# A one-core transformer kernel: the last expert phase fetches an expert's down and up row as one 8 KB row, in groups of four ranks over eight places

## What is computed

```python
def one(args):                      # 128 tokens at a time
    hh, ee, gg = args               # tokens, expert numbers, gates
    a = jnp.einsum("tkd,td->tk", peer_down[ee], hh)
    act = (gg * jax.nn.gelu(a)).astype(hh.dtype)
    return jnp.einsum("tk,tkd->td", act, peer_up[ee])
```

## Time and profile before

| | us |
|---|---|
| median of three runs | 3842.82 |
| lowest and highest run | 3831.79, 3847.68 |
| span of the profiled execution (its own time) | 3996.2 |
| x1's expert phase in it, first gather to the first use of the last sum | 2140.55 to 2909.40 |
| mean DMA rate in that stretch | 359 GB/s |

### The profile page before, as it was taken

One profiled execution on the slowest core, in us unless ns is written; L12 is line 12 of the kernel. 1 busy time (PEld: TensorE's weight loads), 2 busy tenths in 40 slices (PEclk: granted clock), 3 DMA queues, 4 the chain that ended last, 5 costly groups with the idle time before them and its releaser, 6 DMA issues. The chain is left out here.

```text
span 3996.2 us, 45598 instructions
## 1 busy us (share of the span) xinstructions
PE 2820.0 (71%) x15322; PEld 1797.2 (45%) x15322; DVE 2411.0 (60%) x5173; ACT 925.2 (23%) x2085; POOL 1518.1 (38%) x1757
## 2 busy tenths in 40 slices
PE   5999676778664545676686534434489979999999
PEld 2587332324341231222254200000079869798798
DVE  3445788455558776455456776565455766565565
ACT  2432111220111111111131100111133633334433
POOL 0001566665646656666503666666600000000000
PEclk7999887888877777788888766777689989999999
DMA  7666999999989999999926999999955315555444
GB/s 282 251 252 230 361 393 379 383 375 378 388 333 352 372 353 356 376 381 389 376 72 244 363 357 366 365 356 363 366 184 190 128 69 189 173 191 173 153 160 158
DMA packets 274190, 1157.02 MB, mean 290 GB/s; under 512 B 31057, under 2 KB 31825, under 8 KB 235602
## 3 DMA queue, kind: packets, MB, share of 16 engines
q0 software_dynamic: 221184, 805.40, 52.9%
q1 hardware_dynamic: 52818, 349.25, 24.2%
HBM read 1153.49 MB, written 1.05 MB: 289 GB/s over the span
## 5 line engine op out<-in xcount | busy, mean ns | idle before, releaser
L1181 PE MATMUL ps<-rows,diag 128*32 128x512 f32 x3072 | 830.4, 779 | 891.5 <-DMA rows<-in_peer_up,iup 701.7
L2242 DVE CUSTOM_DVE_ANT_0 rows<-rows,ps 128x1024 f32<-128x1024 f32 x768 | 924.6, 1220 | 512.9 <-DMA rows<-in_peer_down,idown 416.3
L2731 POOL DMA_INDIRECT rows<-in_peer_down,idown x768 | 732.7, 954 | 548.6 <-PE ps L1181 322.9
L2731 POOL DMA_INDIRECT rows<-in_peer_up,iup x768 | 732.0, 953 | 318.0 <-issue 208.4
L1181 PEld LDWEIGHTS ps<-rows,diag 128*32 128x32 f32 x3072 | 141.3, 125 | 1519.8 <-DMA rows<-in_peer_up,iup 1214.0
L1243 PE MATMUL ps<-hT_hi,w_hi 128*128 128x256 f32 x1792 | 508.7, 284 | 9.1 <-DVE hT_lo L2383 9.1
L1245 PE MATMUL ps<-hT_lo,w_hi 128*128 128x256 f32 x1792 | 508.3, 284 | 0.0
L1244 PE MATMUL ps<-hT_hi,w_lo 128*128 128x256 f32 x1792 | 506.4, 283 | 0.0
L2806 POOL TENSOR_TENSOR ss<-nwt,minus_half 128x1 f32<-128x1 f32 x24 | 13.2, 551 | 1075.2 <-DVE nwt L1956 1075.2
L1243 PEld LDWEIGHTS ps<-hT_hi,w_hi 128*128 128x128 f32 x1792 | 343.2, 192 | 14.6 <-issue 13.6
L1244 PEld LDWEIGHTS ps<-hT_hi,w_lo 128*128 128x128 f32 x1792 | 342.7, 191 | 0.1
(11 more groups left out here) (327 smaller groups left out, 3899.1 us busy)
## 6 DMA issues: line engine op xcount, KB each, us to landing
wring<-in_wgu SPq DMA_DIRECT2D x66, 1024.0 KB
wring<-in_wdn SPq DMA_DIRECT2D x33, 1024.0 KB
wring<-in_wG SPq DMA_DIRECT2D x32, 1024.0 KB
wring<-in_wmod SPq DMA_DIRECT2D x29, 1024.0 KB
wring<-in_wpq SPq DMA_DIRECT2D x24, 1024.0 KB
rows<-in_wgu SPq DMA_DIRECT2D x22, 1024.0 KB, 4.9
rows<-in_wmod SPq DMA_DIRECT2D x19, 1024.0 KB, 7.6
rows<-in_peer_down,idown POOLq DMA_INDIRECT x768
```

Of the source, the lines that this page charges most:

```text
L1181: ins = pe.matmul(ps[qd:qd + QUAD, UPB + half, :], quad_w[:, j, :], rows[:, j, half * 512:(half + 1) * 512], start=(first and j < QUADS), ...
L2242: dve.tensor_tensor_reduce(out=rows[:, j, :], in0=rows[:, j, :], in1=h_ps, scale=1.0, scalar=0.0, op0=ALU.mult, op1=ALU.add, accum_out=a8[ ...
L2731: pool.indirect_dma_start(out=rows[:, j, :], out_offset=None, in_=table, in_offset=bass.IndirectOffsetOnAxis(ap=offs[:, j:j + 1], axis=0)) ...
```

## The change

- A new input table `peer1` holds layer 1's down and up row of an expert side by side (2048 numbers, 8 KB). In x1's phase one indirect DMA per rank fetches 128 of these rows (1 MB).
- Eight places of 8 KB (`both`): four in `rows`, three in `kvmem`, one in `h[1]` (the context's vectors). Groups of four ranks use places 0 to 3 and 4 to 7 in turn; a place is free again when the ups of its rank are done (`both_up`).
- DVE computes four downs, the gelu and the gates of four ranks (`both_downs`); ACT makes four full 128 x 128 diagonals (`both_diags`); PE multiplies a full diagonal with each half of the up row (`both_ups`), one group behind.
- Ranks are not moved among the partitions in x1 any more: the `moved` stages, the masked copies `sent`, the `move` products and the offset copies on POOL fall away there.
- Loops are written out in x1's phase. Stages that lay beside the first or second half of a group of eight now follow the DVE and ACT work of the first or second group of four; on PE they come ahead of the ups of the group before.
- The gain of the first feed-forward layer has another place; x0 and c0 are unchanged but for the tables' shapes.

```diff
+        both = [rows[:, 2 * n:2 * n + 2, :].rearrange("p a n -> p (a n)") for n in range(HALF)]
+        both += [kvmem[:, n * 2 * D:(n + 1) * 2 * D] for n in range(3)] + [h[1][:, :, :].rearrange("p t n -> p (t n)")]
...
+            def both_ups(i):
+                first, last = i % FOURS == 0, i % FOURS == FOURS - 1
+                if first:
+                    pe.wait_ge(sum_read, GATHER_NO["x1", i // FOURS])
...
+                for j in range(HALF):
+                    pe.wait_ge(both_diag, HALF * i + j + 1)
+                    s = HALF * (i % 2) + j
+                    for half in range(2):
+                        ins = pe.matmul(ps[:, UPB + half, :], diag[:, s, :], both[s][:, D + half * 512:D + (half + 1) * 512],
+                                        start=(first and j == 0), stop=(last and j == HALF - 1))
+                    ins.then_inc(both_up, 1)
...
+                if run == "x1":
+                    for part_, stages in enumerate((beside_a, beside_b)):
+                        i = FOURS * t + 2 * n0 + part_
+                        run_stages(stages)
+                        if i:
+                            both_ups(i - 1)
...
+            def both_diags(i):
+                cols = slice(HALF * (i % 2), HALF * (i % 2) + HALF)
+                act.wait_ge(both_g, 2 * i + 2)
+                act.activation(th8[:, cols], g2[:, cols], ACT.Tanh, scale=GELU_C).then_inc(both_tanh, 1)
+                act.wait_ge(both_act, 2 * i + 2)
+                for j in range(HALF):
+                    s = HALF * (i % 2) + j
+                    if i >= 2:
+                        act.wait_ge(both_up, HALF * (i - 2) + j + 1)
+                    act.activation(diag[:, s, :], ident[:, :], ACT.Copy, scale=act8[:, s:s + 1]).then_inc(both_diag, 1)
...
+            def both_downs(t, n):
+                i = FOURS * t + n
...
+                for j in range(HALF):
+                    c = HALF * (i % 2) + j
+                    dve.wait_ge(both_in[c], 16 * (i // 2 + 1))
+                    dve.tensor_tensor_reduce(out=both[c][:, 0:D], in0=both[c][:, 0:D], in1=h_ps, scale=1.0, scalar=0.0,
+                                             op0=ALU.mult, op1=ALU.add, accum_out=a8[:, c:c + 1]).then_inc(both_down, 1)
...
+            def gather_both(t):
+                for k in range(P):
...
+                    no, c = P * t + k, k % GROUP
+                    if no >= GROUP:
+                        pool.wait_ge(both_up, no - GROUP + 1)
+                    pool.indirect_dma_start(out=both[c], out_offset=None, in_=A["peer1"],
+                                            in_offset=bass.IndirectOffsetOnAxis(ap=idx[t][:, k:k + 1], axis=0)).then_inc(both_in[c], 16)
```

More of the change, by code:

```diff
@@ L33 @@
 HALF = GROUP // 2
+FOURS = P // HALF
 SLOTS = 3
@@ L78, in routes @@
 def routes(r, t, ks):
-    return [st for k in ks for st in [("route", r, t, k, 0), ("route", r, t, k, 1)] + [("moved", r, t, k)] * (k >= 8)]
+    return [st for k in ks for st in [("route", r, t, k, 0), ("route", r, t, k, 1)] + [("moved", r, t, k)] * (k >= 8 and r != "x1")]
 SETS = [[(0, 1), (1, 2), (2, 4), (4, 8)], [(0, 4), (4, 8)]]
 RANKS = [(0, 8, 1, 9, 2, 3, 10, 4, 5, 6, 7, 11), (0, 1, 2, 3, 8, 4, 5, 6, 7, 9)]
-SENDS = [(run, t, 8 + n) for run, t in GATHERS for n in range(len(SETS[t]))]
+SENDS = [(run, t, 8 + n) for run, t in GATHERS if run != "x1" for n in range(len(SETS[t]))]
 def set_mark(t, n):
@@ L135, in during @@
             m = n + 1
-            if not mine[2 * n] and not mine[2 * n + 1]:
+            if r != "x1" and not mine[2 * n] and not mine[2 * n + 1]:
                 while m < GROUPS and not mine[2 * m] and not mine[2 * m + 1]:
@@ L663, in build @@
             "idx_copied", "gelu_step", "gelu_in", "gelu_th", "act_ready", "diag_ready"))
+        both_in = [sem(f"both_in{n}") for n in range(GROUP)]
+        both_down, both_up, both_g, both_tanh, both_act, both_diag = (sem(n) for n in ("both_down", "both_up", "both_g", "both_tanh", "both_act", "both_diag"))
         slot_ok, exp_half, sum_read = sem("slot_ok"), sem("exp_half"), sem("sum_read")
@@ L2232, in gather @@
                 G = GATHER_NO[run, t]
+                if run == "x1":
+                    for part_, stages in enumerate((beside_a, beside_b)):
+                        both_downs(t, 2 * n0 + part_)
+                        run_stages(stages)
+                    return
                 def down(g, first=False):
@@ L2797, in gather @@
                     up(GROUPS - 1, 1, True)
-            for run, t in GATHERS:
-                gather(run, t)
+            def gather_both(t):
+                for k in range(P):
+                    if k % TOP == 0 and (sets := [n for n, (h0, _) in enumerate(SETS[t]) if TOP * h0 == k]):
+                        at_mark(pool, "route", "x1", set_mark(t, sets[0]))
+                    no, c = P * t + k, k % GROUP
[3 more added lines that the diff above has]
+                                            in_offset=bass.IndirectOffsetOnAxis(ap=idx[t][:, k:k + 1], axis=0)).then_inc(both_in[c], 16)
+            for run, t in GATHERS:
+                if run != "x1":
+                    gather(run, t)
+            pool.wait_ge(upp_done, 4 * P)
+            for t in range(TT):
+                gather_both(t)
             pool.memset(minus_half[:, :], -0.5).then_inc(half_set, 1)
```

79 lines of the change are left out of this document (56 added, 23 removed).

## The result

| | us |
|---|---|
| kernel before, median of five runs | 3837.84 |
| changed kernel, median of five runs (lowest, highest) | 3860.86 (3851.18, 3871.61) |
| ratio | 1.0051, 95% interval 1.0034 to 1.0068 |
| span of the profiled execution of the changed kernel | 3862.2 |
| x1's phase in it, first gather to the first use of the last sum | 2043.38 to 2776.70, 733.3 |

The change makes the kernel 0.5% slower where 3803 us, 1.0% faster, was forecast. The interval excludes 1, so the small loss is clear of noise. The profile alone seems to tell another story: its phase is 35 us shorter than the 768.9 of before, and near the forecast 728.2. But its phase also begins at 2043.38 where it began at 2140.55, after stages that the change leaves alone. So the two profiles were not comparable, and the first question is what an execution of the kernel before that takes 3840 us looks like.

What follows compares the result with a forecast made beforehand. The prediction took x1's expert phase as bound by DMA transfers with a small part of starvation. Its terms, 686.0 + 18.8 + 9.8 + 6 + 8.6 - 1.0, gave 728.2 us against 768.9, scaled to 3803 us, range 3755 to 3842.

Steps and rivals of the forecast that it cites:

- The baseline: Whole kernel: median is 0.9616 of the profiled span of 3996.2 us, so -40.7 us there becomes -39, 3803 us.
- The sum itself: x1's expert phase: ranks, side loads, start, DVE's lag and tail add up to 728.2 us, against 768.9 before.
- Starvation: x1's steady part before the change: the queue runs thin at share 0.97, where the best stretches reach 1.03.
- A place comes free in time: x1's groups of four: place free 4.9 us after last landing, new bytes at 7.9, queue dry at 10.7, 2.8 in hand.
- The clock: PE's bursts in x1: even starting each at half speed after about 3 us idle costs nothing or tenths of a us.
- Packets: x1's gathers: 8 KB packets at 335 ns and share 1.00, so 2.68 us a rank and 686.0 us for 256 ranks.
- cut rows: Rival in x1's gathers: rows are cut in two, 349 ns for 8 KB, 2.79 us a rank, 3830 us; chance 0.08.
- Tail: End of x1's phase: 10.5 us from last landing to first sum where it was 1.2, less 0.7, so +8.6 us.
- The thin queue: Rival in x1's transfers: share stays at 0.965, a rank takes 2.777 us, 3828 us; chance 0.10.
- Memory: Rival in x1's transfers: the mean rate is what memory gives to scattered rows, only the tail is added, 3850 us; chance 0.06.
- Half clock: Rival in x1's full products: PE stays at 1.2 GHz through the bursts, 3.74 us a rank, 4043 us; chance 0.05.
- Slow packets: Rival in x1's gathers: 8 KB packets take 395 ns, 3.16 us a rank, 3919 us; chance 0.05.

Runs made afterwards that it cites:

- A: Kind of chip in the follow-up runs: two chips on which the kernel before takes 3842 and 3846 us.
- B: Kind of chip in the follow-up runs: two chips on which the kernel before takes 4016 and 3994 us (one, two sets of runs) and 3992 us (the other).
- the pairs: Changed kernel with groups of two ranks instead of four from rank 56 of the first tile on: 0.9947 of the kernel before on A, 0.9792 to 0.9824 on B.
- e14_in_order: Changed kernel with two 4 KB gathers a rank, fetching x1's table rows in order instead of at random: 3995.2 us on B, 1.0006 of the kernel before.
- e18_pairs_fourth: Changed kernel with groups of two ranks instead of four from rank 56 of the first tile on: 3826.4 us on A, 0.9947 of the kernel before.

## Why the prediction was wrong

- **The baseline**, its largest error and the step that failed. The step was "The median is 0.9616 of that span; with the same share the change is -39". The 153 us between span and median were no even stretch: 63 lay in this phase (768.9 against 706.2), and they were most of what the change could win. The prediction called the scale rough, yet gave no rival for it. On A the same sum has to begin at 706.2: its 728.2 is then 22 us more, or 3860 to 3865 from the medians 3838 and 3843, and 3861 was measured.
- **The sum itself** came out at 728.2 where 733.3 (A) and 731.0 (B) were measured. That is partly luck: on B the ranks and side loads took 714.7 in place of 704.8, and start and tail 16.4 in place of 23.4. On B the forecast of -40.7 stands beside -42.
- **Starvation.** "A small part of starvation", share 0.97 against 1.03, was read as a property of the kernel. On A the share was 1.02 before, so there was hardly any starvation to remove. The rows 3 with 414 GB/s showed the rate that was possible; a median 153 us under the profiled span was a hint that most executions come nearer to it.
- **A place comes free in time.** Forecast 4.9 us from last landing to a free place, measured 6.7 (2396.74 to 2403.41): the first rank of PE's burst took 3.93 for 1.87, what comes before it a little less than forecast. From the issue to the row's landing 0.95 + 2 + 2.68 = 5.6 us were forecast, and 7.8 measured: the first bytes came about when forecast, the whole row later. And the queue lasts 4 x 2.48 = 9.9, not 10.7, as rows move faster than the forecast 2.68 when they move. So the row landed 14.5 us behind the last one, where 12.4 would have lost nothing: "2.8 us in hand" was 2.1 us lacking in this group, and about 1 us in the mean of all. Hence share 0.97, not 1.00.
- **The clock.** "That costs nothing or tenths of a us" counted when the ranks were done, with the two mis-sized terms above beside it. The gap of 3 us was 3.4 to 5.5 ahead of every second burst, these began at the lower level, and that costs 26.5 us. "Even if it fell every time" was more than what happened, and yet it didn't stay free.
- **Packets.** 8 KB packets: right, so cut rows fall. 335 ns forecast, 331 measured, 321 in the pairs; but two of 4 KB are 333 without the late steps, not 349, so the size of the row itself gives at most 4%.
- **Tail** +8.6 forecast, +10.5 measured (11.7 less 1.2): right in kind, 2 short. **DVE's start**: start and tail together are 6.9 + 11.7 = 18.6, where the forecast had 9.8 + 6 + 8.6 - 1.0 = 23.4.
- **The lower edge.** 2.48 us a rank in the same sum gives 675 and -94, not "about -105"; nothing hangs on it.
- **The rivals.** The thin queue, given 0.10, is what happened, at its share of 0.965; its 3828 came from the wrong baseline. Memory falls: up to 413 GB/s over 500 us. That its 3850 lies nearest to 3861 is chance. Half clock through whole bursts falls: the second place is free 1.71 us behind the first, 0.43 for each product row. Slow packets fall.

## What to carry over

Compare a profiled span with the median before anything is taken from it: where they differ by 4%, the difference sits somewhere, and a change that works on just that stretch is worth all of it on one chip and less than nothing on another. In a ring of places the sum that decides is last landing, chain, free place, issue, landing, at the engine's clock after its own idle time; fewer places per turn (two ranks, not four) gave 40 us of this phase, where one row in place of two, with the same late start, gave 20. And a busy share of the DMA engines near 1 doesn't say that they are full: look at the rate.

## What the runs showed of the hardware

- The same kernel takes 3842 and 3846 us on two chips and 3992 to 4016 on two others, one of them met twice. In the profiles of 3996 and 3840 us the loss sits in the phases with 4 KB gathers: 3 us before the first of them, 90 in the two first expert phases, 63 in this one (362 against 401 GB/s), nothing behind. 8 KB gathers reach 385 and 412 GB/s on both. The order of rows in memory has no part in it (e14_in_order); POOL's issuing or the packet count may.
- The Trainium skill, page DMA: Bandwidth & Descriptors, section Specifications, gives about 358 GB/s as HBM's limit for one core, half of what two cores have together. This kernel runs on one core, and e18_pairs_fourth moves 412 over 500 us: the figure doesn't bound it, and the measurement decides.
- A gather of 128 rows of 8 KB issued into a queue that is running dry is at DVE 7.8 us after POOL begins to issue it, its first bytes at most 3.1 us after; in a full queue rows follow one another every 2.48 us.
- In the changed kernel the granted clock was 0.50 from the start of a burst, or from within 1 us of it, where PE had been idle for 3.4 to 5.5 us before. Bursts behind at most 1.9 us of idle ran at the higher level.
